# One pass over the experts by blocks of four keys, with running sums kept in SBUF

## The reference

```python
q = (x @ w_pq)...                       # 8 heads, two halves of 128
s1, s2 = q0 @ k_sub1.T, q1 @ k_sub2.T   # 128 keys each
...                                     # top 16 of the 128 x 128 pairs per head, softmax -> wts
act = gelu(einsum('nhed,nd->nhe', u_exp[idx], x))
out = einsum('nhe,nhed->nd', wts * act, v_exp[idx])
x = x + gate2 * rms_norm(out, g_post_ffn)
```

## Time and profile before

| | us |
|---|---|
| three runs | 5494.3, 5518.67, 5520.8 |
| the profiled execution, its own time | 5503.21 |
| its span, from first to last instruction | 5501.5 |
| the experts on TensorE, first pass | 3149.7 to 4785.4 |
| second pass, to the end of its last matmul | 4785.4 to 5444.4 |
| what follows | 5444.4 to 5501.5 |

### The profile page before, as it was taken

One profiled execution on the slowest core, in us unless ns is written; L12 is line 12 of the kernel. 1 busy time (PEld: TensorE's weight loads), 2 busy tenths in 40 slices (PEclk: granted clock), 3 DMA queues, 4 the chain that ended last, 5 costly groups with the idle time before them and its releaser, 6 DMA issues. The chain is left out here.

```text
span 5501.5 us, 61371 instructions
## 1 busy us (share of the span) xinstructions
PE 5006.1 (91%) x23369; PEld 4094.4 (74%) x23369; DVE 3414.9 (62%) x4458; ACT 1734.2 (32%) x2282; POOL 1392.0 (25%) x1039
## 2 busy tenths in 40 slices
PE   8989999999998898997984599999999999988985
PEld 3347888888886646886874499989999998866764
DVE  7842211214766253233569878888888878878898
ACT  6853112122223111222325433323333233223332
POOL 0500000000000131000006624333334333445453
PEclk9989999999999999998997799999999999999998
DMA  9842232233332474324302799999999999999998
GB/s 360 321 160 91 98 107 90 97 101 106 100 117 94 157 261 165 117 81 158 107 16 64 193 367 378 371 367 385 382 375 389 378 367 371 389 381 406 409 407 344
DMA packets 455580, 1324.25 MB, mean 241 GB/s; under 512 B 135229, under 2 KB 192445, under 8 KB 372719
## 3 DMA queue, kind: packets, MB, share of 16 engines
q1 hardware_dynamic: 333300, 661.82, 34.4%
q0 software_dynamic: 94976, 618.45, 28.6%
q10 hardware_dynamic: 27072, 40.91, 2.1%
HBM read 1200.82 MB, written 121.32 MB: 240 GB/s over the span
## 5 line engine op out<-in xcount | busy, mean ns | idle before, releaser
L227 PE MATMUL ps<-w_hi,act_hi 128*128 128x512 f32 x3040 | 1200.9, 395 | 35.1 <-DVE w_lo L222 16.1
L229 PE MATMUL ps<-w_hi,act_lo 128*128 128x512 f32 x3040 | 1189.6, 391 | 0.0
L228 PE MATMUL ps<-w_lo,act_hi 128*128 128x512 f32 x3040 | 1189.0, 391 | 0.0
L222 DVE TENSOR_TENSOR w_lo<-w_stage,w_hi 128x2048 fp32r<-128x2048 f32 x152 | 348.3, 2291 | 1107.8 <-ACT w_hi L218 1106.8
L2409 ACT ACTIVATE x_hi<-x_stage 128x1024 fp32r<-128x1024 f32 x512 | 543.4, 1061 | 1499.0 <-DMA x_stage<-u_turned 720.4
L2499 DVE TENSOR_TENSOR x_lo<-x_stage,x_hi 128x1024 fp32r<-128x1024 f32 x512 | 626.3, 1223 | 369.2 <-ACT x_hi L2409 368.1
L2336 POOL DMA_INDIRECT u_ring<-u_exp,idx_all x256 | 594.4, 2322 | 836.2 <-DVE u_ring L2517 792.1
L2363 PE MATMUL ps<-act_hi,x_hi 128*128 128x384 f32 x2048 | 694.9, 339 | 61.0 <-DVE x_lo L2499 59.4
L2363 PE MATMUL ps<-x_hi,cx_hi 128*128 128x512 f32 x1536 | 611.9, 398 | 99.0 <-DVE cx_lo L2510 79.9
L227 PEld LDWEIGHTS ps<-w_hi,act_hi 128*128 128x128 f32 x3040 | 574.9, 189 | 159.1 <-DVE w_lo L222 16.4
L2364 PE MATMUL ps<-act_lo,x_hi 128*128 128x384 f32 x2048 | 692.2, 338 | 0.0
(11 more groups left out here) (320 smaller groups left out, 5615.6 us busy)
## 6 DMA issues: line engine op xcount, KB each, us to landing
x_stage<-u_turned SPq DMA_DIRECT2D x256, 512.0 KB, 8.8
x_stage<-v_exp SPq DMA_DIRECT2D x256, 512.0 KB, 9.0
w_stage<-w_ada SPq DMA_DIRECT2D x96, 1024.0 KB, 6.4
w_stage<-w_in SPq DMA_DIRECT2D x96, 1024.0 KB, 5.2
d_w<-w_buf SPq DMA_DIRECT2D x6, 4096.0 KB, 20.7
gwr<-d_w SPq DMA_DIRECT2D x128, 192.0 KB, 11.0
d_gw<-gob ACTq DMA_DIRECT2D x128, 192.0 KB, 7.3
gwr<-d_gw SPq DMA_DIRECT2D x128, 192.0 KB, 10.3
```

The lines of the kernel that those rows point to most:

```text
L222: dve.tensor_tensor(w_lo[:, q % 2], w_in_st[:, q], w_hi[:, q % 2].bitcast(F32), ALU.subtract).then_inc(w_split, 1)
L227: pe.matmul(out, lhs[0], rhs[0], start=first, stop=False)
L228: pe.matmul(out, lhs[0], rhs[1], start=False, stop=False)
L229: return pe.matmul(out, lhs[1], rhs[0], start=False, stop=last)
```

## The change

There is one pass. Each key has four items: two of U, and two of V, both of which use coefficients that stay in SBUF (six places, shared in memory by `gob` and `cx_lo`; five for `cx_hi`). `d_gw` is gone, with the write, the read back and the second split of the coefficients. The V items go in blocks of four keys: keys 0 to 3 with one half of the columns, keys 0 to 3 with the other, keys 4 to 7 with that same half, keys 4 to 7 with the first again, and so on. So the six banks change halves once per four keys (`SWAPS` = 32), and each time VectorE adds them to a sum in SBUF (`put_by`). The staging ring has six places, and `x_lo` is written over `x_stage` in place, so that a place is freed when TensorE has used it. `u_ring` and `v_ring` have three places each. VectorE plays dots and adds alternately, four per key from key 4 on. At the end the norm is in halves: four adds are left, the squares of a half that is finished go ahead, the multiplication by `post` stands before the one by the inverse root.

Constants and the order of items:

```diff
+    RUN = 4
+    SWAPS = NKEY // RUN
     DEPTH = 4
-    RING = 4
+    RAW = 6
+    RING = 3
     NB = 8
+    C_HI, C_LO, GWR = 5, 6, 3
...
+    VSTEPS = 2 * NKEY
...
     def u_item(n, j):
 
-        return 2 * n + j + max(0, n - LAGV)
-
...
+        return 2 * n + j + 2 * max(0, n - LAGV)
+
+    def v_item(v):
+
+        n = LAGV + v // 2
+        return 2 * min(n + 1, NKEY) + 2 * (n - LAGV) + v % 2
+
+    def key_of(v):
+
+        return v // (2 * RUN) * RUN + v % RUN
+
+    def half_of(v):
+
+        return (v // (2 * RUN) + v // RUN) % 2
+
+    def last_use(k):
+
+        return v_item(k // RUN * 2 * RUN + RUN + k % RUN)
+
+    events = []
+    for s in range(NS):
+        events.append(("dot", s))
+        if s >= LAG:
+            events.append(("add", s - LAG))
+    events += [("add", s) for s in range(NS - LAG, NS)]
+
+    def events_before(n):
+
+        return 2 * min(n, LAGV) + 4 * max(0, min(n, NKEY) - LAGV) + max(0, n - NKEY)
```

The rings:

```diff
-        stg = sb(st, "x_stage", [P, 3, UNIT])
         w_hi = sb(st, "x_hi", [P, DEPTH, UNIT], F32R)
-        w_lo = sb(st, "x_lo", [P, DEPTH, UNIT], F32R)
+        raw_at = -(-nc.sbuf_base // 32) * 32
+        stg = sb(st, "x_stage", [P, RAW, UNIT])
+        w_lo = at_sb("x_lo", [P, RAW, UNIT], F32R, offset=raw_at)
         u_ring = sb(st, "u_ring", [P, RING, D])
...
+        f_sum = sb(st, "f_sum", [P, ND, D])
+        c_more = sb(st, "cx_hi", [P, C_HI - 1, DN], F32R)
+        c_hi = [c_more[:, n] for n in range(C_HI - 1)] + [c_one[:]]
```

SyncE:

```diff
             def load_item(i, src):
-                if i >= 3:
-                    sp.wait_ge(lo_done, i - 2)
-                sp.dma_start(stg[:, i % 3], src).then_inc(st_in[i % 3], 16)
-
...
+                if i >= RAW:
+                    sp.wait_ge(pe_used, i - RAW + 1)
+                sp.dma_start(stg[:, i % RAW], src).then_inc(st_in[i % RAW], 16)
...
-                    load_coefs(n)
+                    if n >= GWR:
+                        sp.wait_ge(gw_done, n - GWR + 1)
+                    sp.dma_start(gwr[:, n % GWR], d_w[n]).then_inc(gwr_in[n % GWR], 16)
                 if n >= LAGV:
-                    load_v(n - LAGV)
...
+                    for v in (2 * (n - LAGV), 2 * (n - LAGV) + 1):
+                        load_v(v)
```

TensorE:

```diff
-            def add_up(m):
-                i, first, last = v_item(m), m % NKEY == 0, m % NKEY == NKEY - 1
+            def add_up(v):
+                i, k = v_item(v), key_of(v)
+                first = v == 0 or v % (2 * RUN) == RUN
+                last = v == VSTEPS - 1 or v % (2 * RUN) == RUN - 1
                 pe.wait_ge(lo_done, i + 1)
-                pe.wait_ge(clo_done, m + 1)
+                pe.wait_ge(clo_done, k + 1)
                 for t in range(ND):
                     for hb in range(2):
-                        if m == NKEY:
-                            pe.wait_ge(ev_done, 2 * t + hb + 1)
+                        if first and v > 0:
+                            pe.wait_ge(ev_done, v // (2 * RUN) * BANKS + 2 * t + hb + 1)
...
-                    add_up(n - LAGV)
-            for m in range(NKEY, 2 * NKEY):
-                add_up(m)
+                    add_up(2 * (n - LAGV))
+                    add_up(2 * (n - LAGV) + 1)
```

ScalarE:

```diff
-                if n >= 3:
-                    act.wait_ge(clo_done, n - 2)
-                    act.wait_ge(s_gw[n % 3], 16 * (n // 3))
-                act.activation(gob[:, n % 3], ps[:, n % 2, 0:DN], ACT.Gelu).then_inc(gelu_done, 1)
-
-            def keep(n):
-                act.wait_ge(gw_done, n + 1)
-                act.dma_start(d_gw[n], gob[:, n % 3]).then_inc(s_gw[n % 3], 16)
+                if n >= C_LO:
+                    act.wait_ge(pe_used, last_use(n - C_LO) + 1)
...
+                act.wait_ge(gw_done, m + 1)
+                if m >= C_HI:
+                    act.wait_ge(pe_used, last_use(m - C_HI) + 1)
...
+            def ask_last():
+
+                act.wait_ge(pe_used, u_item(NKEY - 1, 1) + 1)
+                act.wait_ge(f3_out, 16)
+                act.dma_start(f3[:], d_f3).then_inc(f3_in, 16)
+                act.dma_start(post[0][:], d_post[0:1].broadcast_to([P, D])).then_inc(p_in[0], 16)
+                for t in order[:ND]:
+                    act.dma_start(x_rows[t], d_x2[t * P:(t + 1) * P, :]).then_inc(x_in[t], 16)
+                for j in range(STREAMS):
+                    act.dma_start(post[1][j * ST_TOK:(j + 1) * ST_TOK],
+                                  d_post[1 + j:2 + j].broadcast_to([ST_TOK, D])).then_inc(p_in[1], 16)
...
+                if 1 <= n < NKEY + 1:
+                    gelu(n - 1)
+                if 2 <= n < NKEY + 2:
+                    coef_high(n - 2)
...
+                    high(v_item(2 * (n - LAGV)))
+                    high(v_item(2 * (n - LAGV) + 1))
+                if n == NKEY + 1:
+                    ask_last()
```

VectorE in the pass:

```diff
+            def put_by(s):
+
+                side = s % 2 * UNIT
+                dve.wait_ge(pe_used, v_item(s * 2 * RUN + RUN - 1) + 1 if s < SWAPS else N)
+                for t in range(ND):
+                    for hb in range(2):
+                        kept = f_sum[:, t, side + hb * NCOL:side + (hb + 1) * NCOL]
+                        bank = ps[:, 2 + 2 * t + hb]
+                        if s < 2:
+                            dve.tensor_copy(kept, bank).then_inc(ev_done, 1)
+                        else:
+                            dve.wait_ge(ev_done, (s - 2) * BANKS + 2 * t + hb + 1)
+                            dve.tensor_tensor(kept, bank, kept, ALU.add).then_inc(ev_done, 1)
 
             for n in range(STEPS):
                 if n < NKEY:
                     low(u_item(n, 0))
-                if 2 <= n < NKEY + 2:
-                    weigh(n - 2)
-                gathered(n, 0, 2)
+                gathered(n, 0)
...
+                if 1 <= n < NKEY + 1:
+                    weigh(n - 1)
+                if 2 <= n < NKEY + 2:
+                    coef_low(n - 2)
...
+                    v = 2 * (n - LAGV)
+                    if v % (2 * RUN) == RUN:
+                        put_by(v // (2 * RUN))
+                    low(v_item(v))
+                    gathered(n, 1)
+                    low(v_item(v + 1))
+                else:
```

VectorE at the end:

```diff
-            more(2)
-            dve.wait_ge(s_sd, 1)
-            dve.reciprocal(ss[:, 0:ND + 1, 3], ss[:, 0:ND + 1, 2]).then_inc(s_rs, 1)
-            more(1)
-            dve.wait_ge(s_rs, 1)
-            for i, t in enumerate(order[:-1]):
-                normed(i, t)
-                more(1)
...
+                dve.wait_ge(s_sq, 3 + t)
+                times_post(f_sum[:, t], 0, second_half)
+            inverse_of(lone, 1)
+            finish(GT[0], f3[:], TT - 1, 1, 1)
+            put_by(SWAPS)
+            dve.wait_ge(s_sq, 4 + ND)
+            times_post(acc, 1, slice(0, D))
+            sum_of(four, 4 + 2 * ND)
+            mean_of(four, 2)
+            for t in range(ND):
+                times_post(f_sum[:, t], 0, first_half)
+            inverse_of(four, 2)
+            for t in range(ND):
+                finish(t, f_sum[:, t], t, 2, 3 + ND + t)
+            finish(TP, acc[:], ND, 2, 2 + ND)
```

More of the change, by code:

```diff
@@ L166, in _build @@
     d_w = dram("d_w", (NKEY, P, DN))
-    d_gw = dram("d_gw", (NKEY, P, DN))
     d_f3 = dram("d_f3", (P, D))
@@ new lines, in half_of, with dots_before @@
+    def half_of(v):
[10 more added lines that the diff above has]
+        return 2 * min(n, LAGV) + 4 * max(0, min(n, NKEY) - LAGV) + max(0, n - NKEY)
+    def dots_before(n):
+        return sum(kind == "dot" for kind, s in events[:events_before(n)])
@@ L2264, in experts @@
-        gwr_in = [sem(f"x_gwr{n}") for n in range(4)]
-        chi_done, clo_done, v_used = sem("x_chi"), sem("x_clo"), sem("x_vused")
+        gwr_in = [sem(f"x_gwr{n}") for n in range(GWR)]
+        chi_done, clo_done = sem("x_chi"), sem("x_clo")
         ev_done = sem("x_ev")
@@ L2272, in experts @@
         p_in = [sem(f"x_p{g}") for g in range(2)]
[L2273 to L2278, removed]
+        s_sq, s_st, s_ms, s_sd, s_rs, s_f, y_done, s_y = (
+            sem("x_" + n) for n in ("sq", "st", "ms", "sd", "rs", "f", "y", "out"))
+        order = [GT[0], *range(ND), TP]
+        x_rows = [None] * TT
+        for i, t in enumerate(order):
+            x_rows[t] = x_more[:, i] if i < ND else u_ring[:, (NS - RING + i - ND) % RING]
         @block.sync
@@ new lines, in _ @@
+            gelu_slots(STEPS)
+            act.wait_ge(gw_done, NKEY)
+            act.wait_ge(f3_in, 16)
+            for c in range(2):
+                square(f3[:, c * UNIT:(c + 1) * UNIT], ss[:, c, TT - 1:TT])
+            act.wait_ge(ev_done, SWAPS * BANKS)
+            for t in range(ND):
+                square(f_sum[:, t, UNIT:], ss[:, 1, t:t + 1])
+            act.wait_ge(s_ms, 1)
+            root(slice(TT - 1, TT))
+            act.wait_ge(added, NS)
+            for c in range(2):
+                square(acc[:, c * UNIT:(c + 1) * UNIT], ss[:, c, ND:ND + 1])
@@ L2561, in _ @@
```

(35 more changed lines are left out.)

207 lines of the change are left out of this document (67 added, 140 removed).

## The result

The changed kernel takes 5350.9 us in the median of four runs (5350.4 to 5355.1), against 5514.3 for the kernel before in the same comparison: a ratio of 0.9715 (95% interval 0.970 to 0.973). The forecast was 5395. The profiled execution took 5350.5 us, its span is 5348.8, so of the old span of 5501.5 us 152.7 are gone, where the sum had 112.

A forecast was written before the change was run, and what follows sets the result against it. TensorE was taken to bound the first pass, not the second, and the new stretch: 2142.7 + 6 + 43 + 5 = 2197 us, saving 98, plus 14 at the end. 5503.2 less 112 gave 5391, forecast as 5395, range 5340 to 5430.

The forecast's parts named there:

- the sum: Whole kernel: new stretch 2142.7 + 6 + 43 + 5 = 2197 us, saving 98, and 14 at the end: 112 us saved.
- Idle time in the flow: TensorE's idle time in the single pass: 2.0% of 2143 = 43 us, bounds nothing and double that share.
- the loads step: Staging loads: issued 20.9 us before TensorE needs the item, 16 us needed, 5 us to spare; gaps should be rarer.
- f_three and h_row: VectorE's mid-pass waits of 8.6 and 6.5 us fall on 5.4 us of slack per four keys: 5 us.
- the start: First score to first V matmul: 6 us lost to the first loads in the old kernel, kept at 6 us.
- The change of banks: put_by once per four keys: 2 us of cover for TensorE, costed at nothing, bounded by 3 us x 31 = 93.
- rival A: DMA is the bound of the new pass: a stretch of 2208 to 2259 us, time 5402 to 5455; chance 0.20.
- Gathers: u_ring and v_ring of three: 19.7 us of cover against landings of 10.8 median, 14.5 or 19.1 at most; no loss.
- rival D: Gathers starve VectorE, slower: a mean wait of 0.55 us per gather eats the gain, 1 us gives 5740; chance 0.10.
- The end: Behind TensorE's last matmul: 43 us in place of 57.1, bounds 39 and 50, 14 us saved.
- The price of a score: TensorE's 48 matmuls of a score take 8.48 us by distance of starts, 128 of them in the pass.

## Why the prediction was right

Direction, mechanism and order of size held: the time fell by 163 us where 124 were forecast, and 5350.9 lies inside the forecast's range of 5340 to 5430, near its low end. TensorE is the bound of one long pass, at 16.76 us per key against 16.74 worked out, with DMA at 388 GB/s as worked out. The terms, by their steps:

- **Idle time in the flow, mis-sized.** I took 2.0%, 43 us, from the first pass as it stood, though the loads step had just said that the ring of three made those gaps and the new lead has 5 us to spare. With f_three and h_row (5 us) that is 48; the flow shows 2061.8 - 123 x 16.74 = 3. The experiment with the ring alone shows why: the gaps belonged to the staging that the change removes. This is the whole miss in the stretch, 45 us, less 3 at the start (8.8 against 6) and 7 behind the last score, where I had none. The row was also misread: up to its last score the first pass has 123 V items and not 124, so its idle time behind the start was 36 us and not 32.
- **The clock, left out.** I put all 6 us of the start down to loads. But the granted clock has a share: 0.93 over the 51.2 us of the changed kernel's start is 3.6 of its 8.8 us, and three waits of TensorE for `x_lo` make 4.9. Behind the last score it cost 1.7 us, beside the wait of 4.9.
- **The change of banks.** Free where a score stands behind it, as costed: 2.7 us of VectorE's waiting were left, where I counted 4.6. Doubling the changes cost 3 us. But I did not look at the one change behind the last score, where the cover of 8.5 us doesn't exist: 4.9 us, the price by my own terms, 0.2 + 3.6 + 1.1, and the slower matmuls behind it. put_by measured 3.68 us for six.
- **DMA and rival A.** 388 GB/s needed, 421 to be had. The doubt came from reading 376 GB/s at a share of 0.98 as a limit; it was what TensorE and the ring asked for. The 358 GB/s of the Trainium skill (DMA: Bandwidth & Descriptors, Specifications) is no bound here: the new pass held 388 for 2062 us. The highest rate of a window shown, 422, stays under the 435 that the same section gives for the fabric. Rival A's times were misadded too: stretches of 2208 to 2259 us are 11 to 62 above my 2197, so 5406 to 5457.
- **Gathers and rival D.** Three places were enough, and in the flow so were two. What failed is the expectation for two places: it let waits of up to 3 us come at every gather, from the longest landing of 14.5 us, while the median of 10.5 lies under its own shortest interval of 12.4.
- **f_three and h_row.** 7.4 and 5.4 us of VectorE's waiting, none of TensorE's in sight.
- **The end.** 39.0 against 43: the last add ended 6.4 us behind TensorE, not 9, and the last output took 5.6.
- **The price of a score.** 8.48 us from the earlier trace rows was nearly right: the mean in the changed kernel is 8.44, by the starts in its trace, 5 us less over 128.

What each part gave, by spans: the staging ring 64 us of the stretch (2294.7 to 2231.1), the single pass with everything else in it 69 (to 2162.0), the end 18. The single pass was not split further: whether it works with the ring of three was not tried.

## What to carry to other kernels

Idle time read from the stretch that a change rewrites must be carried over only after asking which part of it the change removes; here the term was inherited whole and made the miss. A resource at a share of 0.98 may be asked for no more than it gives: adding traffic tells its limit, the share does not. Cover that comes from a neighbour in the order has to be checked at the last turn of the loop, where that neighbour is missing.

## What was not expected of the hardware

DMA went up to 421 GB/s with one core over 2133 us, with busy shares of 1.02, some 45 of it copies from DRAM to DRAM; shares of 0.96 to 0.99 went with rates from 369 to 388. Behind TensorE's wait of 4.9 us the granted clock was 0.57 in the mean of 2.8 us; with a wait of 0.9 us at that place it stayed at 1.00. A gather's landing time hardly moved with the number in flight: 10.8 us median with four places, 10.5 with two.
